# Two transformer blocks on one core: second modulation halves among the first feature tiles, loop quarters one unit on, mixer outputs copied ahead of the context tiles

## The reference, cut to what matters

```python
m  = (silu(c) @ w_ada + b_ada)            # 9 vectors of 1024; mc likewise from c_ctx
x   = x   + 0.5 * m[2]  * swiglu(modulate(rmsnorm(x),   m[0],  m[1]),  w_ffn1_in, w_ffn1_out)
ctx = ctx + 0.5 * mc[2] * swiglu(modulate(rmsnorm(ctx), mc[0], mc[1]), w_ffn1_in, w_ffn1_out)
px = modulate(rmsnorm(x), m[3], m[4]) @ w_mix_in
pc = modulate(rmsnorm(ctx), mc[3], mc[4]) @ w_mix_in
...                                       # attention, convolution, w_mix_out, second swiglu
mod = silu(c_2) @ w_mod + b_mod           # 6 vectors for the second block
h = modulate_2(rmsnorm_2(x), ...) @ w_in  # projections for x and for the context
...                                       # retention, gated linear attention, w_out
u = down[idx]; y = sum_k (g * gelu(u . x)) * up[idx]    # experts, 128 rows per token
```

## Time and profile before

| | |
|---|---|
| time, median of 3 runs | 3087.21 us (3081.78 to 3094.99) |
| time of the profiled execution, and its span | 3088.89 us, 3087.1 us |
| PE busy | 2706.9 us (88%) |
| DVE, ACT, POOL busy | 1730.2, 885.3, 1158.4 us |
| bytes moved | 722.07 MB, mean 234 GB/s |
| granted TensorE clock, mean | 0.967 |

### The profile page before, as it was taken

How to read it: one execution, slowest core, us unless ns; L and a number is a source line. 1 busy time by engine, 2 the same in 40 slices (tenths; PEclk the granted TensorE clock), 3 DMA queues, 4 the chain that set the end, 5 groups by cost and what they waited for, 6 DMA issues and landing times.

```text
span 3087.1 us, 29851 instructions
## 1 busy us (share of the span) xinstructions
PE 2706.9 (88%) x10998; PEld 1863.3 (60%) x10998; DVE 1730.2 (56%) x3649; ACT 885.3 (29%) x1675; POOL 1158.4 (38%) x763
## 2 busy tenths in 40 slices
PE   6999989989989999999978899988777777777876
PEld 4999989977668888688837755543232322232332
DVE  6666662032747613322165577767777776777765
ACT  3111132134532223332142333333222222222221
POOL 1223223224934444323110355545444444444442
PEclk8999999999999999999988999999999999999999
DMA  6455532212025423212100389999999999999996
GB/s 243 161 185 179 166 111 58 61 64 73 22 68 181 161 96 101 84 62 69 51 20 15 137 341 407 405 427 421 427 427 427 427 427 427 427 427 427 427 427 294
DMA packets 125231, 722.07 MB, mean 234 GB/s; under 512 B 14864, under 2 KB 16144, under 8 KB 58288
## 3 DMA queue, kind: packets, MB, share of 16 engines
q0 software_dynamic: 73728, 536.90, 41.6%
q1 hardware_dynamic: 35920, 127.74, 12.0%
q10 hardware_dynamic: 15456, 55.79, 5.6%
HBM read 718.29 MB, written 2.10 MB: 233 GB/s over the span
## 4 chain that ended last, share of the span: by engine, by line
PE 58%; DMA 26%; DVE 9%; ACT 3%; issue 3%; POOL 1%; SPq 0%; ACTq 0%; DVEq 0%; POOLq 0%
PE acc L615 14%; PE acc L616 14%; PE acc L617 14%; DMA hid<-in_peer_rows,squares 9%; DMA wring<-in_peer_rows,squares 7%; DMA resid<-in_peer_rows,squares 5%; PE sums L1104 5%; PE acc L1104 3%; DMA arena<-in_peer_rows,squares 3%; PE sums L548 1%; DMA modw<-in_peer_rows,squares 1%; DVE hid L2477 1%; ACT hid L1163 1%; DVE squares L1883 1%; PE acc L839 1%
## 5 line engine op out<-in xcount | busy, mean ns | idle before, releaser
L2642 POOL TENSOR_TENSOR wring_parts<-wring,wring_parts 128x1024 fp32r<-128x1024 f32 (+1 forms) x215 | 522.5, 2441 | 1192.5 <-ACT wring_parts L1163 1192.3
L615 PE MATMUL acc<-hid_parts,wring_parts 128*128 128x384 f32 (+1 forms) x2152 | 794.8, 369 | 44.6 <-DVE hid_parts L1830 18.2
L617 PE MATMUL acc<-hid_parts,wring_parts 128*128 128x384 f32 (+1 forms) x2152 | 776.6, 361 | 0.0
L616 PE MATMUL acc<-hid_parts,wring_parts 128*128 128x384 f32 (+1 forms) x1656 | 597.6, 361 | 0.0
L615 PEld LDWEIGHTS acc<-hid_parts,wring_parts 128*128 128x128 f32 x2152 | 407.3, 189 | 111.1 <-issue 48.1
L617 PEld LDWEIGHTS acc<-hid_parts,wring_parts 128*128 128x128 f32 x2152 | 407.0, 189 | 38.6
L1163 ACT ACTIVATE wring_parts<-wring 128x1024 fp32r<-128x1024 f32 (+1 forms) x215 | 223.2, 1040 | 529.5 <-DMA wring<-in_w_ffn_out 200.6
L616 PEld LDWEIGHTS acc<-hid_parts,wring_parts 128*128 128x128 f32 x1656 | 314.5, 190 | 32.7 <-issue 5.5
L2654 POOL DMA_INDIRECT arena<-in_peer_rows,squares x180 | 199.6, 1109 | 224.4 <-PE acc L1104 135.5
L1163 ACT ACTIVATE hid<-hid 128x2 f32<-128x2 f32 (+2 forms) x293 | 67.0, 229 | 755.6 <-DVE arena L2477 229.4
L2654 POOL DMA_INDIRECT wring<-in_peer_rows,squares x158 | 174.3, 1103 | 222.0 <-PE acc L1104 163.5
(11 more groups left out here) (412 smaller groups left out, 4297.8 us busy)
## 6 DMA issues: line engine op xcount, KB each, us to landing
wring<-in_w_ffn_in SPq DMA_DIRECT2D x88, 512.0 KB, 4.8
modw<-in_w_ada ACTq DMA_DIRECT2D x56, 512.0 KB, 3.6
modw<-in_w_mod ACTq DMA_DIRECT2D x48, 512.0 KB, 3.8
wring<-in_w_ffn_out SPq DMA_DIRECT2D x32, 512.0 KB, 3.5
wring<-in_w_in SPq DMA_DIRECT2D x28, 512.0 KB, 3.4
wring<-in_w_mix_in SPq DMA_DIRECT2D x18, 512.0 KB, 3.4
wring<-in_peer_w_q SPq DMA_DIRECT2D x16, 512.0 KB, 5.9
wring<-in_w_ffn_out SPq DMA_DIRECT2D x16, 384.0 KB, 3.1
```

Source lines behind the costliest of these rows:

```text
L615: nc.tensor.matmul(o, wh, high, start=first, stop=False)
L616: nc.tensor.matmul(o, wh, low, start=False, stop=False)
L617: return nc.tensor.matmul(o, wl, high, start=False, stop=last)
L2642: nc.gpsimd.tensor_tensor(Wlor[:, p, 0:blocks, 0:cols], Wlo[:, p, 0:blocks, 0:cols], Whir[:, p, 0:blocks, 0:cols], ALU.subtract).then_inc( ...
```

## The change

It does five things.

- The halves of group 1 are multiplied before `first_units`, behind a wait until ACT has made `rstd` (their bank holds the norm's mean until then), and those of group 3 behind feature tiles 0 and 1. Their turns stand behind tiles 0 and 2 instead of 2 and 3. `first_rows(2)` stands on DVE behind `first_low(0)`.
- The low parts of weight tiles 0 and 1 are made by DVE (`first_weights`), in front of and behind `first_modulation(0)`; POOL begins at tile 2. The two clears of `sums` stand with the others at the start.
- In the loop, DVE's two quarters behind unit u are now 2(u-1) and 2(u-1)+1 from the first unit on; before, quarters 0 and 1 stood ahead of unit 0, and units 1 to 3 did the two after those.
- ACT's loads for the loop stand ahead of the two high parts of an odd unit, for every unit; before, behind them.
- At the mixer and at the projections, ACT copies the first two outputs ahead of the context's shifts. Two high parts that stood between the shifts (mixer) or ahead of the statistics (projections) stand ahead of these copies.

```diff
@@ TensorE
-            pe.wait_ge(banks_zeroed, 3)
+            pe.wait_ge(banks_zeroed, 5)
...
             mod_turn(2, 2)
-            pe.wait_ge(banks_zeroed, 5)
+            pe.wait_ge(rstd_ready, 1)
+            first_half(1, 0)
+            first_half(1, 1)
 
             def behind_feature(k):
 
-                if k < 4:
-                    first_half(1 + 2 * (k // 2), k % 2)
+                if k == 0:
+                    first_half(3, 0)
+                    mod_turn(1, 3)
+                if k == 1:
+                    first_half(3, 1)
                 if k == 2:
-                    mod_turn(1, 3)
-                if k == 3:
                     mod_turn(3, 4)
@@ ScalarE, silus
+                    if halves == 2 and u:
+                        for x in range(first_quarter + 2 * u, min(first_quarter + 2 * u + 2, stop_quarter)):
+                            mod_load(x)
                     if u % halves == halves - 1 and u < units * FT // 2 - 1:
                         for m in range(2):
                             high_part(s0 + W_RING + 2 * (u // halves) + m)
-                    late = 2 if halves == 2 and u >= 4 else 0
-                    for x in range(first_quarter + 2 * u + 2 - late, min(first_quarter + 2 * u + 4 - late, stop_quarter)):
-                        if not (late and u == 4):
+                    if halves == 1:
+                        for x in range(first_quarter + 2 * u + 2, min(first_quarter + 2 * u + 4, stop_quarter)):
                             mod_load(x)
@@ ScalarE, mixer (and the same for the projections with rq, shift(3), shift_context(1))
-            shift(1, hi768r, lo768, 3 * KD, TC, 3, {1: s0 + 2, 4: s0 + 3})
-            shift_context(0, hi768r, lo768, 3 * KD)
+            shift(1, hi768r, lo768, 3 * KD, TC, 3)
...
-            for t in range(4):
+            for t in range(2):
+                high_part(s0 + 2 + t)
+                take("q", t, qT[:, t, :])
+            shift_context(0, hi768r, lo768, 3 * KD)
+            ahead(s0)
+            ahead(s0 + 1)
+            for t in range(2, 4):
                 take("q", t, qT[:, t, :])
                 ahead(s0 + t)
@@ ScalarE, ahead of the projections' stat
-            for s in range(s0 + 2, s0 + W_RING):
-                high_part(s)
@@ VectorE, swiglu
-                if first_pair == 0:
-                    mod_quarter(0)
-                    mod_quarter(1)
...
-                    late = 1 if sides == 2 and u >= 4 else 0
+                    late = sides - 1
...
-                    if pair < stop_pair and (u or first_pair) and not (late and u == 4):
+                    if pair < stop_pair and u >= late:
@@ VectorE, opening
-            for bank in (acc[:, 0, :], acc[:, 1, :], misc[:, :]):
+            for bank in (acc[:, 0, :], acc[:, 1, :], misc[:, :], sums[:, 0, :], sums[:, 1, :]):
                 V.memset(bank, 0.0).then_inc(banks_zeroed, 1)
...
+            def first_weights(s):
+
+                dve.wait_ge(w_high, s + 1)
+                V.tensor_tensor(Wlor[:, s], Wlo[:, s], Whir[:, s], ALU.subtract).then_inc(w_ready, 1)
+
             first_rows(0, acc[:, 0, :])
+            first_rows(1, acc[:, 1, :])
+            first_weights(0)
+            first_modulation(0)
+            first_weights(1)
             stat()
-            for w in range(2):
-                V.memset(sums[:, w, :], 0.0).then_inc(banks_zeroed, 1)
-            first_rows(1, acc[:, 1, :])
-            first_modulation(0)
             first_scale(0)
-            for j in range(1, 4):
-                first_scale(j)
-                first_low(j - 1)
+            first_scale(1)
+            first_low(0)
+            first_rows(2, sums[:, 0, :])
+            first_scale(2)
+            first_low(1)
+            first_scale(3)
+            first_low(2)
             first_low(3)
-            first_rows(2, sums[:, 0, :])
             first_rows(3, sums[:, 1, :])
@@ GpSimd
-            for s in range(TILE_OF["mix_out"]):
+            for s in range(2, TILE_OF["mix_out"]):
                 low_part(s)
```

More of the change, by code:

```diff
@@ L1502, in _ @@
             s0 = TILE_OF["proj"]
-            for s in range(s0 + 2, s0 + W_RING):
-                high_part(s)
             stat(KD, TC, renormed)
             shift(3, hi768r, lo768, ADA_TILES, TC, 4)
-            shift_context(1, hi768r, lo768, ADA_TILES)
             def both(name, s, dst):
@@ L1522, in both @@
                     ahead(s + c + 1)
-            for t in range(4):
+            for t in range(2):
+                high_part(s0 + 2 + t)
+                take("rq", t, rq[:, t, :])
+            shift_context(1, hi768r, lo768, ADA_TILES)
+            ahead(s0)
+            ahead(s0 + 1)
+            for t in range(2, 4):
                 take("rq", t, rq[:, t, :])
```

## The result

The changed kernel takes 3096.07 us (median of 20 runs) where the kernel before takes 3087.07 (20 runs): a ratio of 1.0028, 95% interval 1.0019 to 1.0038. One of the changed kernel's 20 runs took 6907.55 us; the ratio leaves it out. The profiled execution has a span of 3095.3 us against 3087.1, at a mean granted clock of 0.964 against 0.967.

A forecast was written before the change was run, and what follows sets the result against it. PE was taken to bound the loop, with a thin lead. From 3087.2 us: opening -11, mixer -8.3, projections -3 (together -22), loop +33, giving 3098; own range 3089 to 3106, 8-in-10 range 3058 to 3108.

The forecast's parts named there:

- Opening: Start to unit 2: earlier feature tiles, no wait before unit 2, no clock fall; -10.5 to -12.3 us, -11 taken.
- rival 4: Group 3 lands too late, or the context's chain ends late at the mixer; half of the 22 lost, 3109; 5%.
- The hold: Loop: POOL's low parts hold DVE's quarter instructions, so an even unit's quarters end 8.9 us behind its silu.
- Rival 1: Loop: no collision of POOL with DVE's quarters, `mod_add` waits 0 to 0.7, 3059 us; 22%.
- The landing: Loop: the even unit's second load leaves level with the second tile load and takes 6.2 us to land.
- rival 2: Loop: loads behind the tiles take 5.1 us, long wait 2.5 without a clock fall, 3072 us; 15%.
- the completion rule: Loop loads: completion is signalled only after that transfer engine's earlier writes, so order, not source, makes landings late.
- The price: Loop: long and short `mod_add` waits in turn plus low clock cost 42.5 us, less 9.3; net +33 (+24 to +39).
- What went of the old loop: Loop costs that go: 6.1 us at `mod_add`, some 0.2 of waits and 3 of clock; 9.3.
- Rival 3: Loop: low clock doesn't give the lead back, so every `mod_add` costs the long wait; 3121 us; 8%.
- Mixer: Mixer's head: first pair earlier, no wait for ACT's copy, no clock fall; -8.3 us (-7.5 to -9).
- Projections: Projections' head: faster scales and no wait for the copy, part returning at the fifth tile; -3 us (-1.5 to -4).

The follow-up runs named there:

- after_again: The changed kernel, unchanged, profiled a second time; 3098.1 us.
- after_no_hold: The changed kernel with POOL writing zeros in place of the low parts in the first feed-forward loop; 3067.23 us in one run.
- before_loads_ahead: The kernel before with only ACT's two loads put ahead of an odd unit's high parts, from unit 5 on; 3111.18 us, 1.0073 of before.
- after_loads_behind: The changed kernel with ACT's two loads put back behind the high parts; 3069.19 us, 0.9937 of before.
- after_small_load: The changed kernel with every odd quarter's load, from the fourth quarter on, bringing 32 KB instead of 512 KB; 3074.6 us in one run.
- before_heads: The kernel before with only the change's edits at the heads of the mixer and the projections; 3074.19 us, 0.9939 of before.
- before_heads_again: The kernel before with only the mixer's and projections' head edits, timed and profiled a second time; 3077.88 us, 0.9956 of before.
- pool_first_lows: The changed kernel with loads behind the high parts and POOL again making the low parts of weight tiles 0 and 1; 3071.9 us in one run.
- after_highs_between: The changed kernel with an odd unit's two high parts placed between ACT's two loads; 3069.51 us, 0.9943 of before.

## Why the prediction came out near

**Opening: right, with a different reason for the first tile.** Forecast -11; measured -9.7 at the start of unit 2 and -12.05 at its silu. First tile 30.80 (forecast 31.2), fifth 47.44 (48.5), DVE's low part 1.23 (1.2), unit 2's wait 0.18 (0.15). Forecast was that group 1 fits into PE's wait; it fills it: PE begins tile 0 when the second half is done, at 1.89 us a half where the forecast took at most 1.63. In `after_again` PE was done ahead of DVE's low part and waited 1.22 for it. Group 3 arrived in time, so that half of rival 4 fell.

**The hold: right to a tenth.** 8.9 forecast, 8.94 measured, made of the 0.4 that the forecast worked out and of 2.15 as the earlier trace rows had it. Rival 1, no collision, is refuted by the rows above, and `after_no_hold` shows what it would have given: 3067, where the rival had 3059. Of the 8 us between them, 4 are behind the projections, where this execution took 1535.8 us and that of before 1531.6, though no line differs there.

**The landing: right in its place in the chain, its size off.** The forecast put 6.2 us everywhere. Transfers of after issued level with the tile loads at 304.23 and at 320.93, the first from `w_ada`, the second from `w_mod`:

```profile
modw<-in_w_ada ACTq DMA_DIRECT2D x1, 512.0 KB, 5.3
...
modw<-in_w_mod ACTq DMA_DIRECT2D x1, 512.0 KB, 6.4
```

Over all traces, loads of 512 KB that are level with the tile loads (within 0.15 us, behind 70 us) took 4.4 to 6.0 from `w_ada` (23 of them, median 5.1) and 5.4 to 6.8 from `w_mod` (10, median 6.2); so the source makes about 1 us, and the two ranges overlap. Being behind makes about as much: in `after_again` two loads from `w_ada`, 1.1 and 0.4 behind, took 6.31 and 6.39. Up to 310 us all loads are from `w_ada`, and there 0.9 less in each of two places of the cascade shortens the long wait from 5.3 to about 3.5; measured 2.9 to 3.0. With `w_mod` it is 5.4 and 7.9. So rival 2's number, 5.1, was the true one for six tenths of the loop of this trace, but its conclusion (2.5 without a fall of the clock) was wrong on the clock: it fell to 0.51 behind a 2.87 us wait. That the order and not the source makes the price is shown by `before_loads_ahead` and `after_loads_behind`. The prediction's reason for it, the completion rule, is not shown: in `after_small_load` it was the data that moved late.

**The price: 30.7 instead of 33.** By its terms: waits at L600 27.7, forecast 5 x (5.3 + 0.7) = 30. Low clock: from the silu of unit 2 to that of unit 43 after takes 401.26 and `after_no_hold` 362.34; the 38.9 less the 27.7 leave 11.2, forecast 5 x 2.5 = 12.5. So 38.9 in place of 42.5. What went of the old loop: before takes 370.57 for the stretch, so 8.2 against `after_no_hold`, forecast 9.3; and 38.9 - 8.2 = 30.7. In other pairs it is 8.5 to 12.6 (before's three traces 368.4 to 370.6; `before_heads` 359.8 and `before_heads_again` 358.0, neither with a long wait). The mis-sized term is the long wait, too long for `w_ada`; that there were six of them and not five made up for part of it. `after_again` shows that "long and short in turn" is a pattern, not a law; the total is what holds (27.7 and 26.1). The step that the low clock gives ACT and DVE their lead back fits the two traces of the changed kernel, and no run tests it apart. Rival 3's condition, no lead given back, was met where the clock did not fall: behind 3.35 in after and behind 2.73 in `after_again`, and both times the next wait was long. Behind the other waits above 2.5 that another `mod_add` of these two traces follows (2.87, 2.97, 2.90 and 5.41; 2.97, 5.03 and 5.13) it was 0.57 or 0.58. The 1.86 of `after_again` and the 2.76 of `before_loads_ahead` are the two exceptions: there the clock fell, and 1.13 and 1.65 came next.

**Mixer: right.** Forecast -8.3; -7.35 in after and -8.2 in `before_heads`. Over all traces the stretch takes 211.0 to 212.2 with the old head and 203.5 to 205.0 with the new one. DVE's scales are 0.74 each, the third tile has no wait, and the k tile waits 0.94 (forecast 0 to 1.7, 0.9 taken), though for POOL's low part:

```profile
697.59 0.41 PE L615 MATMUL acc<-hid_parts,wring_parts 128*128 128x384 f32 x1 [0.94 <-POOL wring_parts L2660]
```

**Projections: right in size.** Forecast -3. From PE's 2.23 us wait ahead of the head to its 3.5 us wait behind the projections, traces with the old head take 261.1 to 262.0 and those with the new one 258.4 to 259.2; for after against before it is 3.0. The rest of after's 4.6 lies between the mixer and this head (428.8 against 430.3), where no line differs, and where traces with the changed head have 428.6 to 435.2; so those 1.6 are no gain of the change.

**The sum.** Forecast -22 + 33 = +11. In the marks: -12.05 - 7.35 - 4.6 + 30.7 + 2.0 - 0.5 = +8.2, and +9 by the medians. The 2.0 between the loop and the mixer has no term in the forecast: before has 202.4 for this stretch in each of three traces, the others 202.4 to 205.3, and what makes it is open. That the sum came within 2 us is in part luck: the opening gave 1 more than forecast, the loop cost 2 less and the projections' stretch gave 1.6 more, and against them stand the mixer's 1 less and these 2.0. The runs themselves spread wider than any of these (3088.67 to 3103.78 for the changed kernel).

**What was not seen.** The gains don't simply add. The heads alone give 18.1 and 12.7 by the medians (forecast 11), the opening and the quarters 13.6 (forecast 11, inside its interval). All of them together with the loads behind give 19.4 to 19.7, not the sum of these, and the parts without a price had been forecast at 22 + 9.3 - 3.5 = 28 (rival 1). `after_loads_behind` has runs in two clusters, 3060 to 3064 and 3074.6 to 3075.5. Its profile is of the lower one (3061.3), 27.6 us below the profiled execution of before. What makes the upper cluster was in no trace of it; a long wait with its low clock at the end of the loop, as `pool_first_lows` and `after_highs_between` had once each (4.5 and 4.1 us), has about that size, but this is only argued.

## What to carry to other kernels

The order of an idle engine's instructions is a timing of others: ACT had time for loads and high parts in either order, and the order alone moved the whole kernel by 27 us (3096 against 3069), since it set when POOL worked and so when DVE was held. Look in a stretch with "no wait" at how far each partner engine ends ahead of its deadline: 7.3 of 8.25 us was room, 8.9 was not, and behind that edge the late load costs again what the hold cost at first. When gains and a price come in one change, time them apart; here moving three lines turned 9 us lost into 19 won.

## What the runs showed that was not expected

- A 32 KB transfer on ACT's queue reports after 1.6 to 1.8 us when it stands 0.8 us ahead of the 512 KB tile loads of SP's queue, and after 3.8 to 4.5 when it is level with them (within 0.15); 0.3 and 1.3 behind them it took 5.3 and 5.8, and its data packets were late, not its report alone. 512 KB took 3.4 to 5.1 when 0.8 to 1.3 ahead, 4.4 to 6.8 when level, and 4.8 to 6.9 when up to 1.3 behind.
- In the same place transfers from `w_mod` take about 0.2 us longer than those from `w_ada` when alone (medians 3.84 and 3.63), and about 1 longer level with the tile loads (medians 6.2 and 5.1 over all traces, with overlap).
- The granted clock fell to its lower level (1.2 of 2.4 GHz) behind waits of PE at L600 of 1.86, 2.45 and 2.76 to 2.97 us, but not behind one of 2.00, one of 2.73 and one of 3.35. So waits between 1.86 and 3.35 go either way here; all 13 of 3.75 and more, in nine traces, fell.
- A pair of POOL's memsets of 128x1024 takes 1.90 us, a pair of its subtractions 4.7 to 5.2 in the loop of after, and one such subtraction by DVE 1.23.
